# Depthwise conv taps on 32x32 tiles of TensorE, and 64-row score products in column halves

## The chip, the cores and the metric
One core of a Trainium2 chip runs the whole program. The metric is the device time of one execution in microseconds (us). Engines: TensorE (PE in the profile, its weight loads PEld), VectorE (DVE), ScalarE (ACT), GpSimd (POOL), and SyncE (SP), which issues the weight DMAs.

## What is computed
Two transformer blocks on a sequence of 512 tokens, width 1024, all in float32. The first has a hybrid mixer (differential attention with 4 heads of 2 x 64, and "fox" attention with 8 heads of 64 and a forget gate), cross attention to 256 memory tokens, and a squared-ReLU MLP. The second begins with the mixer that the change is about, then cross attention, a gated MLP with a three-tap conv, latent attention, cross attention again and a second gated MLP. The two parts that matter:

```python
def pool_conv_mixer(h, w_in, pool_w, pool_scale, dw_w, dw_b, ln_g, ln_b, w_out):
    z = h @ w_in
    u, glu_a, glu_b = jnp.split(z, [POOL_W, POOL_W + CONV_W], axis=-1)      # 512 each
    ...                                                                     # window means of u, @ pool_w -> ya
    gl = glu_a * jax.nn.sigmoid(glu_b)
    cv = causal_dwconv(gl, dw_w) + dw_b                                     # 31 taps, one channel each
    yb = jax.nn.silu(layernorm(cv, ln_g, ln_b))
    return jnp.concatenate([ya, yb], axis=-1) @ w_out
```

```python
s1 = jnp.einsum('bhqd,bhkd->bhqk', sl(qa1), ka1).astype(jnp.float32) * scale + rel    # d = 64, causal
s2 = jnp.einsum('bhqd,bhkd->bhqk', sl(qa2), ka2).astype(jnp.float32) * scale + rel
sb = jnp.einsum('bhqd,bhkd->bhqk', sl(qb), kb).astype(jnp.float32) * scale + ...      # fox, d = 64
```

## The kernel before
Everything lies feature-major: 128 features on the partitions, 512 tokens along the free axis. A dense product is split in three (mm3, L964): hi times hi, hi times lo, lo times hi of the operands, each a fast fp32r matmul of 512 columns. ScalarE writes the hi part of each 1 MB weight block (`hi`, L1628), GpSimd the lo part in four pieces (`low_part`, L810), SP loads the raw block two ahead. Other matmuls (scores, attention values, sums over features by a matrix of ones, conv taps) are plain f32.

Results go to PSUM through two rings of four banks each, L for dense products and S for the rest. `make_plan` writes down, in the order of the program, which engine frees each bank: "v" VectorE, "a" ScalarE. TensorE claims a bank (`claim`) when the group four places before has been read. There is no scheduler: each engine runs its instructions in the order in which its function writes them, and semaphores hold it where it must wait.

**The pool and conv mixer** is the stretch from about 950 to 1110 us. Its 512 conv channels are four chunks of 128 (`gl[:, q]`). A tap is a shift of the tokens times one weight per channel. TensorE does a tap of a whole chunk as a 128x128 diagonal matrix times the shifted chunk, summed in PSUM (L1470, L1485). VectorE does one as a fused multiply-add in SBUF (`taps`, L2783).
- Chunks 0 and 1: all 31 taps on VectorE. Chunk 2 (`SHARED_Q`): taps 0 to 14 on VectorE, 15 to 30 on TensorE ("conv2"). Chunk 3 (`PE_Q`): all on TensorE ("conv3"). So 77 taps on VectorE, 47 on TensorE. `tap_order` mixes VectorE's chunks, so that two taps of one chunk rarely follow one another.
- ScalarE makes the 47 diagonals (`diags` L2067, `shared_diags` L2074).
- TensorE's order: glu (8 groups of 128 features), pool_u (4 groups, two blocks), xk1+ (keys of the next cross attention, 256 columns), conv3, pool_w (4 products), conv2, first half of pc_out_a, ln_mean, second half, ln_var, memory values, pc_out_b. ln_mean (L1495) waits for all taps.
- VectorE's order: the glu scaling (`glu_in`, L2314), gates (`glu`, L2756), the normalised residual (L2763), scaled pool_u (L2314), the four window sums (L2803), means (L2808) and subtraction (L2811, which counts `pool_r` for pool_w), the lows of pool_w's results (L2818, for which pc_out_a waits), the closing adds of conv3 and conv2 (L2824, L2829). Taps stand between them.

The rows of the later sections also show L2884 (the three-tap conv of the gated MLP, whose taps wait each for the one before), L1601 (values of the latent attention: for each key tile k, two heads e, each a 128x64 product into its own half of a bank's partitions), L2157 (ScalarE's copy of 64 partitions out of PSUM) and L1309 (the causal mask, bf16, added by a matmul).

**The score products.** `diff_score` (L1263) and `masked_scores` (L1307) make two products at a time: head part 0 from partitions 0 to 63, part 1 from 64 to 127, each 64 rows x 128 columns of weights, moving 128 to 512 columns, into two banks. Each of the two attention stages has 16 such pairs, with dense products between them.

```python
            for j in range(CONV_K):
                pe.wait_ge(diag_r, j + 1)
                ins = pe.matmul(bank(S, g)[:, :], diag(j), gl[:, PE_Q, j:j + T], start=j == 0, stop=j == CONV_K - 1)
```

## Time and profile before

| | |
|---|---|
| median of 3 runs | 2385.51 us (2381.87 to 2385.61) |
| the profiled execution: its time, its span | 2383.48 us, 2381.6 us |
| granted TensorE clock, mean | 0.997 |
| PE busy | 2348.1 us (99%), 10762 matmul records |
| DVE, ACT, POOL busy | 1218.8, 939.8, 997.2 us |

The profile is one execution. A row of a timeline gives the start, the length up to the end of the last instruction of the group, engine, line, operation, output and inputs, shape and count. "128*128 128x512" is 128 rows by 128 columns of weights, and a moving operand of 128 partitions x 512 elements. Records of PE are pipelined: a matmul's record is longer than the step to the next one. A row of a list of groups ends with busy us and mean ns, then the engine's idle time before the group and what ended it.

### The profile page before, as it was taken

Reading aid. Unit: us, or ns where it says so; the run is one execution under the profiler, and the core shown is the slowest. Engines: PE = TensorE matmul, PEld = TensorE weight load, DVE = VectorE, ACT = ScalarE, POOL = GpSimd, SP = SyncE. Lnnn points to the kernel's source line nnn. Section 1 sums busy time; section 2 is a strip of 40 time slices with the busy share of each in tenths; the row PEclk is TensorE's granted clock in tenths of the full one; section 3 lists DMA queues with packets and bytes.
Section 4 is the critical chain, followed back from the end, with each engine's and each line's share of the span. In section 5 each row is a group of like instructions: output and inputs, shape, how many; then the busy total and the mean of one; then the engine's idle time right before and its main releaser. Section 6 shows DMA issues by size and latency. Waiting matters only on the chain.

```text
span 2381.6 us, 29066 instructions
## 1 busy us (share of the span) xinstructions
PE 2348.1 (99%) x10762; PEld 1864.9 (78%) x10762; DVE 1218.8 (51%) x2026; ACT 939.8 (39%) x1418; POOL 997.2 (42%) x744
## 2 busy tenths in 40 slices
PE   8999999999999999999999999999999999999999
PEld 6777778878888888757878888887667877888887
DVE  4454545244433346794457555556774243655544
ACT  3355444334222227424444222225875443322222
POOL 4323335223544545635525545444113233545443
PEclk9999999999999999999999999999999999999999
DMA  5212322422323223223213232222013521332231
...
DMA packets 170087, 218.69 MB, mean 92 GB/s; under 512 B 6585, under 2 KB 144107, under 8 KB 169975
## 3 DMA queue, kind: packets, MB, share of 16 engines
...
## 4 chain that ended last, share of the span: by engine, by line
PE 89%; DVE 4%; ACT 3%; issue 1%; POOL 1%; DMA 1%; SPq 0%; DVEq 0%; ACTq 0%
PE ps_l L964 79%; PE ps_l L1383 2%; PE ps_l L1113 1%; PE ps_s L1366 1%; ACT w_hi L1628 1%; POOL w_lo L810 1%; PE ps_s L1470 1%; DVE small L3025 1%; DVE arena L3017 1%; PE ps_s L1485 1%; PE ps_s L1263 1%; PE ps_s L1307 0%; PE ps_s L964 0%; DVE small L3027 0%; PE ps_l L1248 0%
## 5 line engine op out<-in xcount | busy, mean ns | idle before, releaser
L810 POOL TENSOR_TENSOR w_lo<-w_raw,w_hi 128x512 fp32r<-128x512 f32 (+1 forms) x740 | 997.0, 1378 | 1363.2 <-ACT w_hi L1628 1340.5
L964 PE MATMUL ps_l<-a_hi,w_hi 128*128 128x512 f32 x1936 | 762.9, 394 | 3.9 <-POOL w_lo L810 2.9
L964 PE MATMUL ps_l<-a_lo,w_hi 128*128 128x512 f32 x1952 | 758.4, 389 | 0.0
L964 PE MATMUL ps_l<-a_hi,w_lo 128*128 128x512 f32 x1936 | 754.0, 389 | 0.0
L1628 ACT ACTIVATE w_hi<-w_raw 128x2048 fp32r<-128x2048 f32 (+2 forms) x196 | 370.6, 1891 | 598.5 <-PE ps_l L964 575.7
L964 PEld LDWEIGHTS ps_l<-a_hi,w_hi 128*128 128x128 f32 x1936 | 362.7, 187 | 89.9 <-issue 10.9
L964 PEld LDWEIGHTS ps_l<-a_lo,w_hi 128*128 128x128 f32 x1952 | 365.9, 187 | 78.4 <-issue 3.1
L964 PEld LDWEIGHTS ps_l<-a_hi,w_lo 128*128 128x128 f32 x1936 | 362.7, 187 | 76.9
L964 PE MATMUL ps_l<-b_hi,w_hi 128*128 128x512 f32 (+1 forms) x892 | 330.3, 370 | 6.7 <-issue 2.3
L964 PE MATMUL ps_l<-b_lo,w_hi 128*128 128x512 f32 (+1 forms) x892 | 327.3, 367 | 0.0
L964 PE MATMUL ps_l<-b_hi,w_lo 128*128 128x512 f32 (+1 forms) x892 | 327.2, 367 | 0.0
L964 PEld LDWEIGHTS ps_l<-b_hi,w_hi 128*128 128x128 f32 x892 | 168.5, 189 | 38.0 <-issue 3.1
L964 PEld LDWEIGHTS ps_l<-b_hi,w_lo 128*128 128x128 f32 x892 | 168.6, 189 | 27.6
L964 PEld LDWEIGHTS ps_l<-b_lo,w_hi 128*128 128x128 f32 x892 | 168.6, 189 | 27.4 <-issue 0.2
L2910 DVE TENSOR_TENSOR x_T<-ps_l,x_T 128x512 f32<-128x512 f32 x160 | 109.3, 689 | 44.6 <-PE ps_l L964 42.6
L2314 DVE TENSOR_TENSOR arena<-ps_l,rst 128x512 f32<-128x512 f32 x56 | 38.2, 689 | 171.6 <-PE ps_l L964 114.9
L2715 DVE TENSOR_TENSOR x_T<-ps_l,x_T 128x512 f32<-128x512 f32 x120 | 82.9, 691 | 59.0 <-PE ps_l L964 58.0
L2627 DVE TENSOR_TENSOR x_T<-ps_l,x_T 128x512 f32<-128x512 f32 x64 | 43.5, 688 | 118.8 <-PE ps_l L964 118.5
L1660 ACT ACTIVATE a_hi<-x_T,cols 128x512 fp32r<-128x512 f32 x64 | 46.2, 723 | 141.4 <-DVE x_T L2627 141.4
L2875 DVE TENSOR_TENSOR arena<-ps_l,rst 128x512 f32<-128x512 f32 x44 | 30.4, 692 | 134.3 <-PE ps_l L964 121.2
L2691 DVE SCALAR_TENSOR_TENSOR arena<-ps_l,rst 128x512 f32<-128x512 f32 x32 | 22.0, 691 | 146.6 <-PE ps_l L964 137.3
L2884 DVE SCALAR_TENSOR_TENSOR arena<-arena,cols 128x512 f32<-128x512 f32 x88 | 91.3, 1038 | 8.4 <-DVE arena L2880 0.3
...
## 6 DMA issues: line engine op xcount, KB each, us to landing
...
```

Of the source, the lines that this page charges most:

```text
L810: e.tensor_tensor(w_lo[:, b % 2, o], w_raw[:, b % 2, o], w_hi[:, b % 2, o].bitcast(F32), ALU.subtract).then_inc(w_lo_made[by], 1)
L964: ins = pe.matmul(o, *((v, w) if swap else (w, v)), start=first and n == 0, stop=last and n == 2)
L1113: return pe.transpose(o, v, ident)
L1383: ins = pe.matmul(bank(L, g)[:, :], vM[:, m, h * 256 + d * P:h * 256 + (d + 1) * P], ptx(h)[:, m, :], start=m == 0, stop=m == MT - 1)
L1628: act.activation(w_hi[:, b % 2, 0:size], w_raw[:, b % 2, 0:size], ACT.Copy).then_inc(w_hi_made, 1)
L1660: act.activation(z_of(k)[0][:, n, :], x[:, n, :], ACT.Copy, scale=gain(k, n)).then_inc(n_hi, 1)
L2314: dve.tensor_tensor(dst(j), bank(L, g + j)[:, :], rst if r is None else r, ALU.mult)\
L2627: dve.tensor_tensor(x[:, n, :], bank(L, g)[:, :], x[:, n, :], ALU.add).then_inc(l_free["v"], 1)
L2715: dve.tensor_tensor(x[:, n, :], bank(L, g + n)[:, :], x[:, n, :], ALU.add)\
L2875: dve.tensor_tensor(gp[:, c, 2:T + 2], bank(L, g + c)[:, :], rst, ALU.mult)\
L2884: dve.scalar_tensor_tensor(out=cv[:, c, :], in0=gp[:, c, j:T + j], scalar=wcol(cw + 22 * j, k, i), in1=cv[:, c, :], op0=ALU.mult, op1=ALU. ...
L2910: dve.tensor_tensor(x[:, n, :], bank(L, g + n)[:, :], x[:, n, :], ALU.add)\
```

## The change
The conv: `tap_order` goes. VectorE keeps chunk 0 alone (31 taps in a row); TensorE takes chunks 1, 3 and 2, in this order, one before each pool_u block and one after them. A tap of a chunk is four f32 matmuls of 32 rows x 32 columns of weights, one for each 32 channels, whose diagonal blocks (`diag(n)`) VectorE builds for all 31 taps of a chunk in one instruction out of a 128x32 stack of small identities. Tap j sends channels 32r.. to bank s = (j+1) mod 4 and, in it, to the partitions of quarter (r + s) mod 4. So 16 matmuls in a row use 16 different tiles of the array, each with its own bank and quarter. The sum over the four banks and the way back to the right quarter is then made by ScalarE (12 copies of 32 partitions, banks 1 to 3, `conv_out`) and VectorE (`conv_add`, three adds). A chunk takes all four S banks; its adds come ahead of a given point of VectorE's order, and the copies for a chunk wait for the adds of the one before. ScalarE makes no diagonals any more.

The scores: both banks of a pair are claimed first; each 64x128 product becomes two of 64x64, for query columns 0 to 63 and 64 to 127.

```diff
--- before.py
+++ after.py
@@ -368,8 +368,8 @@
     feat("xk1+", "xa_wkv_2:0", "a", [768])
     L.add("pool_w", "vvvv")
     feat("pc_out_a", "pc_w_out_2", "v", [0, 512], nk=4, width=512)
-    S.add("conv3", "v")
-    S.add("conv2", "v")
+    for q in PE_CHUNKS:
+        S.add(f"conv{q}", "vaaa")
     S.add("ln_mean", "v")
     S.add("ln_var", "a")
...
@@ -424,27 +424,8 @@
...
-PE_Q = 3
-SHARED_Q, SHARED_TAPS = 2, 15
...
+DVE_CHUNK = 0
+PE_CHUNKS = (1, 3, 2)
...
@@ -677,10 +659,13 @@
         pool_wt = ar(12800, 4, P)
         ly = ar(R0, 4, T)
 
-        def diag(j):
-
-            o = P * j if j < 24 else R0 + 2168 + P * (j - 24)
-            return arena[:, o:o + P]
+        def diag(n):
+
+            return arena[:, 32 * CONV_K * n:32 * CONV_K * (n + 1)].rearrange("p (j c) -> p j c", c=32)
+
+        def conv_part(s):
+
+            return ar(10752 + T * (s - 1), T)
 
         qh, vh, kh = ar(R0, 8, T), ar(10752, 4, T), ar(HALF, 8, T)
         cosT, sinT = ar(12800, T), ar(13312, T)
@@ -1259,9 +1245,12 @@
                 n = P * (i + 1)
                 for s in (0, 1):
                     claim(pe, S, g + s)
+                for s in (0, 1):
                     r = slice(64 * s, 64 * s + 64)
-                    pe.matmul(bank(S, g + s)[:, 0:n], qa[r, h, i * P:(i + 1) * P], ka[r, h, 0:n],
-                              start=True, stop=True).then_inc(s_full, 1)
+                    for o in (0, 64):
+                        ins = pe.matmul(bank(S, g + s)[o:o + 64, 0:n], qa[r, h, i * P + o:i * P + o + 64], ka[r, h, 0:n],
+                                        start=True, stop=True)
+                    ins.then_inc(s_full, 1)
 
             def diff_subln(g, h):
                 claim(pe, S, g)
@@ -1302,9 +1291,11 @@
             def masked_scores(g, i, both):
 
                 n = P * (i + 1)
+                for e in (0, 1):
+                    claim(pe, S, g + e)
                 for e, (q, k) in enumerate(both):
-                    claim(pe, S, g + e)
-                    pe.matmul(bank(S, g + e)[:, 0:n], q, k[:, 0:n] if n < T else k, start=True, stop=False)
+                    for o in (0, 64):
+                        pe.matmul(bank(S, g + e)[o:o + 64, 0:n], q[:, o:o + 64], k[:, 0:n], start=True, stop=False)
                 for e in (0, 1):
                     pe.matmul(bank(S, g + e)[:, i * P:n], ident_bf[:, :], mask_bf[:, :], start=False, stop=True)\
                         .then_inc(s_full, 1)
@@ -1460,17 +1451,30 @@
...
             stage("glu", xa, ready=h_ready(4), behind={0: both_sums})
-            stage("pool_u", xa, nb=2)
+            def conv_taps(n):
+
+                q = PE_CHUNKS[n]
+                g = S.base[f"conv{q}"]
+                pe.wait_ge(glu_r, q + 1)
+                pe.wait_ge(diag_r, n + 1)
+                for s in range(4):
+                    claim(pe, S, g + s)
+                for j in range(CONV_K):
+                    s = (j + 1) % 4
+                    for r in range(4):
+                        rows, out = slice(32 * r, 32 * r + 32), 32 * ((r + s) % 4)
+                        ins = pe.matmul(bank(S, g + s)[out:out + 32, :], diag(n)[rows, j, :], gl[rows, q, j:j + T],
+                                        start=j < 4, stop=j >= CONV_K - 4)
+                    if j >= CONV_K - 4:
+                        ins.then_inc(s_full, 1)
+
+            b, g = plan.block_base["pool_u"], L.base["pool_u"]
+            conv_taps(0)
+            feat(b, g, 8, 256, xa)
+            conv_taps(1)
+            feat(b + 1, g + 2, 8, 256, xa)
+            conv_taps(2)
             stage("xk1+", xm, nb=1, n=MEM)
-            g = S.base["conv3"]
-            claim(pe, S, g)
-            pe.wait_ge(glu_r, 4)
-            for j in range(CONV_K):
-                pe.wait_ge(diag_r, j + 1)
...
@@ -1478,19 +1482,12 @@
...
-            g = S.base["conv2"]
-            claim(pe, S, g)
-            for j in range(SHARED_TAPS, CONV_K):
...
             feat(b, g, 4, 512, lambda k: xa(4 + k), lambda k: wait_read(pe, L, L.base["pool_w"] + k))
             g = S.base["ln_mean"]
             claim(pe, S, g)
-            pe.wait_ge(tap, TAPS)
-            wait_read(pe, S, S.base["conv2"])
+            pe.wait_ge(tap, CONV_K)
+            pe.wait_ge(conv_sum, len(PE_CHUNKS))
...
@@ -2059,20 +2056,20 @@
...
-            def diags():
-                for j in range(CONV_K):
...
+            def conv_out(n):
+
+                if n:
+                    act.wait_ge(conv_sum, n)
+                for s in (1, 2, 3):
+                    g = S.base[f"conv{PE_CHUNKS[n]}"] + s
+                    wait_group(act, S, g)
+                    for r in range(4):
+                        c = (r + s) % 4
+                        ins = act.activation(conv_part(s)[32 * r:32 * r + 32, :], bank(S, g)[32 * c:32 * c + 32, :], ACT.Copy)
+                    ins.then_inc(s_free["a"], 1)
+
+            for r in range(0, P, 32):
+                act.activation(part_id[r:r + 32, :], ident[r:r + 32, r:r + 32], ACT.Copy).then_inc(part_id_r, 1)
...
@@ -2081,10 +2078,13 @@
                     wait_read(act, L, g + 4 * pair + 2 + c)
                     act.activation(sgb[:, c, :], sgb[:, c, :], ACT.Sigmoid).then_inc(sg_r, 1)
                 hi(b + 2 * pair + 3)
-            diags()
-            just_hi("pool_u", 2)
+            b = plan.block_base["pool_u"]
+            conv_out(0)
+            hi(b + 2)
+            conv_out(1)
+            hi(b + 3)
+            conv_out(2)
             block_copies("xk1+", 1, 2, lambda j: kT[:, 6 + j, :], cols=MEM)
-            shared_diags()
             for q in range(4):
                 wait_group(act, L, L.base["pool_w"] + q)
                 act.activation(A_hi[:, 4 + q, :], bank(L, L.base["pool_w"] + q)[:, :], ACT.Copy,
@@ -2769,39 +2769,61 @@
...
             glu_in(1, 0)
+            dve.wait_ge(part_id_r, 4)
+            for n, q in enumerate(PE_CHUNKS):
+                w = COL["conv_dw_w_2"] + q
+                dve.tensor_tensor(diag(n), part_id.unsqueeze(1).broadcast_to((P, CONV_K, 32)),
+                                  cols[:, w:w + 4 * CONV_K - 3:4].unsqueeze(2).broadcast_to((P, CONV_K, 32)), ALU.mult)\
+                    .then_inc(diag_r, 1)
 
...
             def taps(upto):
-                for n in range(tap_n[0], min(upto, TAPS)):
-                    j, q, before = TAP_ORDER[n]
+                q = DVE_CHUNK
+                for j in range(tap_n[0], upto):
                     w = col("conv_dw_w_2", 4 * j + q)
                     if j == 0:
                         ins = dve.tensor_scalar(cvt[:, q, :], gl[:, q, 0:T], w, col("conv_dw_b_2", q), ALU.mult, ALU.add)
                     else:
-                        dve.wait_ge(tap, before + 1)
+                        dve.wait_ge(tap, j)
                         ins = dve.scalar_tensor_tensor(out=cvt[:, q, :], in0=gl[:, q, j:j + T], scalar=w,
                                                        in1=cvt[:, q, :], op0=ALU.mult, op1=ALU.add)
                     ins.then_inc(tap, 1)
-                tap_n[0] = max(tap_n[0], min(upto, TAPS))
+                tap_n[0] = upto
+
+            def conv_add(n):
+
+                q = PE_CHUNKS[n]
+                g = S.base[f"conv{q}"]
+                wait_group(dve, S, g)
+                wait_read(dve, S, g + 1)
+                dve.scalar_tensor_tensor(out=cvt[:, q, :], in0=bank(S, g)[:, :], scalar=col("conv_dw_b_2", q),
+                                         in1=conv_part(1), op0=ALU.add, op1=ALU.add).then_inc(s_free["v"], 1)
+                wait_read(dve, S, g)
+                wait_read(dve, S, g + 2)
+                dve.tensor_tensor(cvt[:, q, :], cvt[:, q, :], conv_part(2), ALU.add).then_inc(conv_acc, 1)
+                dve.wait_ge(conv_acc, n + 1)
+                wait_read(dve, S, g + 3)
+                dve.tensor_tensor(cvt[:, q, :], cvt[:, q, :], conv_part(3), ALU.add).then_inc(conv_sum, 1)
 
             glu(0)
-            taps(8)
             glu_in(1, 1)
-            taps(18)
+            taps(1)
             glu(1)
             normed_x(range(4, KD))
+            taps(4)
+            conv_add(0)
             scaled(L.base["pool_u"], 2, lambda j: up_[:, j, 16:UW], r34)
-            taps(26)
+            taps(12)
+            conv_add(1)
             scaled(L.base["pool_u"] + 2, 2, lambda j: up_[:, 2 + j, 16:UW], r34)
...
                 step(dve.tensor_tensor(dst[:, 0:m, st:UW], src[:, 0:m, st:UW], src[:, 0:m, st - d:UW - d], ALU.add))
-                taps(28 + 4 * (n + 1))
+                taps(12 + n + 1)
                 sync()
...
@@ -2810,7 +2832,8 @@
...
-            taps(60)
+            taps(20)
+            conv_add(2)
...
@@ -2818,17 +2841,7 @@
...
-            taps(TAPS)
-            g = S.base["conv3"]
...
+            taps(CONV_K)
             def pool_out(ns):
...
```

## Rows read from the trace of the kernel before

**Rows 1.** the page: span, busy time of the engines
```profile
span 2381.6 us, 29066 instructions
...
PE 2348.1 (99%) x10762; PEld 1864.9 (78%) x10762; DVE 1218.8 (51%) x2026; ACT 939.8 (39%) x1418; POOL 997.2 (42%) x744
```

**Rows 2.** busy time by stretches, pool projection to mean (columns: first line)
```profile
core 0: us, PE busy (x) PEld busy (x) DVE busy (x) ACT busy (x) POOL busy (x), PEclk, DMA share, GB/s
995.40:1023.60 28.20, 28.09 (x146) 23.40 (x145) 28.16 (x32) 16.23 (x37) 21.15 (x11) 1.00 0.31 105
...
1067.00:1078.30 11.30, 11.30 (x51) 9.18 (x50) 10.19 (x16) 0.00 (x0) 0.00 (x0) 1.00 0.00 0
sum 82.90, PE 82.79 PEld 51.73 DVE 81.72 ACT 27.25 POOL 32.45; mean PE 16.56 PEld 10.35 DVE 16.34 ACT 5.45 POOL 6.49
```

**Rows 3.** the list of waits, PE, 950 to 1130 us: total us, times, longest
```profile
PE ps_l L964 <- POOL w_lo L810: 0.8, 3, 0.3
```

**Rows 4.** timeline of PE: start us, us, line, op, tiles, count
```profile
1023.57 26.78 PE L1470 MATMUL ps_s<-arena 128*128 128x512 f32 x62
...
1053.62 13.90 PE L1485 MATMUL ps_s<-arena 128*128 128x512 f32 x32
1066.96 0.79 PE L964 MATMUL ps_l<-a_hi,w_hi 128*128 128x512 f32 x1
...
1078.25 3.17 PE L1495 MATMUL ps_s<-arena,ones 128*128 128x512 f32 x7
```

**Rows 5.** busy time of line L1601 alone, 1699.19 to 1701.50 us
```profile
1699.19:1701.50 2.31, 2.30 (x16) 1.06 (x16) 1.00 0.00 0
```

**Rows 6.** line L1601 at 1699.2 and to 1699.7: ns min/median/max, starts
```profile
L1601 PE MATMUL ps_l<-arena x2: 643/643/643, 1699.2 to 1699.2; 128*64 128x512 f32 x2
...
L1601 PE MATMUL ps_l<-arena x4: 592/618/643, 1699.2 to 1699.7; 128*64 128x512 f32 x4
```

**Rows 7.** line L1263, 95.13 to 95.2 and 95 to 95.5 us
```profile
L1263 PE MATMUL ps_s<-arena x2: 373/373/373, 95.1 to 95.1; 64*128 64x128 f32 x2
...
L1263 PE MATMUL ps_s<-arena x4: 272/322/373, 95.1 to 95.4; 64*128 64x128 f32 x4
```

**Rows 8.** timeline of PE around a score pair, 301 to 303.5 us
```profile
302.41 0.92 PE L1307 MATMUL ps_s<-arena 64*128 64x384 f32 x4
303.26 0.28 PE L1309 MATMUL ps_s<-mask_bf,ident_bf 128*128 128x128 bf16 x2
```

**Rows 9.** timeline of DVE, 979 to 1060 us
```profile
979.12 0.69 DVE L2314 TENSOR_TENSOR arena<-ps_l,arena 128x512 f32<-128x512 f32 x1 [1.52 <-PE ps_l L964]
984.56 0.69 DVE L2314 TENSOR_TENSOR arena<-ps_l,arena 128x512 f32<-128x512 f32 x1 [4.75 <-PE ps_l L964]
...
988.38 7.16 DVE L2783 SCALAR_TENSOR_TENSOR arena<-arena,cols 128x512 f32<-128x512 f32 x6
...
1049.52 10.68 DVE L2783 SCALAR_TENSOR_TENSOR arena<-arena,cols 128x512 f32<-128x512 f32 x16
```

**Rows 10.** groups by line and shape, DVE, 980 to 1080 us
```profile
L2811 DVE SCALAR_TENSOR_TENSOR arena<-arena 128x512 f32<-128x512 f32 x4 | 2.5, 687 | 0.0
...
L2803 DVE TENSOR_TENSOR arena<-arena 128x1042 f32<-128x1042 f32 x1 | 1.2, 1230 | 0.0
```

**Rows 11.** timeline of DVE in the gated MLP's three-tap conv
```profile
1390.21 1.65 DVE L2884 SCALAR_TENSOR_TENSOR arena<-arena,cols 128x512 f32<-128x512 f32 x2
```

**Rows 12.** busy time of line L2803, the window sums, 1025 to 1046 us
```profile
1025.00:1046.00 21.00, 7.11 (x4) 1.00 0.31 101
```

**Rows 13.** groups by line, ACT, 990 to 1095 us
```profile
L1628 ACT ACTIVATE w_hi<-w_raw 128x2048 fp32r<-128x2048 f32 x6 | 11.4, 1908 | 36.6 <-PE ps_l L964 36.6
L2067 ACT ACTIVATE arena<-keep,cols 128x128 f32<-128x128 f32 x31 | 9.2, 391 | 0.0
```

**Rows 14.** groups by line and shape, ACT, whole span
```profile
L2157 ACT ACTIVATE arena<-ps_l 64x512 f32<-64x512 f32 x16 | 9.5, 593 | 6.7 <-PE ps_l L964 6.6
```

**Rows 15.** the list of waits, PE, 60 to 330 us
```profile
PE ps_s L1263 <- ACT arena L1736: 0.4, 1, 0.4
```

44 lines of the change are left out of this document (3 added, 41 removed).

## Prediction

> **What bounds the kernel now.** The first part of the page shows TensorE (PE) busy 99% of a 2381.6 us span, the next engine 51% [rows 1]. So the kernel is TensorE's own stream of work, and an edit counts by what it takes out of that stream, as long as nothing else then holds it up. Next I read the busy time by stretches from the pool projection to the layer norm's mean [rows 2]. PE is busy in 82.8 of 82.9 us, at granted clock 1.00 (the 2.4 GHz level). What the page's averages hide is the DVE column: 81.7 of 82.9 us. In this stage two engines are full, and VectorE is the one that a faster PE would meet. The list of waits confirms that PE now waits for nothing there: 0.8 us in 180 us [rows 3]. The PE timeline gives the pieces: conv3 from 1023.57, conv2 from 1053.62, the first half of pc_out_a from 1066.96, ln_mean at 1078.25 [rows 4].
>
> **The convolution on PE.** 31 tap matmuls leave 62 records [rows 4]: an f32 matmul is two passes, each its own weight load and multiply. They run 26.78 us, of which the last lies 0.59 in its own, so the start-to-start of a 512-column pass is 26.2/61 = 0.43 us and a tap 0.86. Removed: conv3 62 x 0.43 = 26.6 and conv2 1053.62 to about 1067.1 = 13.5, together 40.1 us for 47 taps.
> Added: 93 taps in four 32x32 matmuls each, 372 matmuls, 744 passes and as many weight loads. Sixteen successive matmuls (four taps) lie on sixteen different tiles, so with all of them at work at once four taps cost 2 passes = 0.86 us. A chunk is 8 rounds: 6.9 us. Nothing in this trace uses 32x32 tiles; the nearest rows use two tiles. For the 128x64 products of the latent attention, 16 passes of 4 x (512+384+256+128) columns would take 4.3 us in a row at 0.43 per 512 and took 2.31, and the first two records, 512 columns each, start in the same 0.1 us [rows 5, 6]. They belong to two different matmuls, for a second pass of the first could not start before 0.43. Two 64-row tiles start together likewise [rows 7]. So both ways to split the array run side by side, at full rate, and a later matmul passes the second pass of an earlier one. I take that to hold for sixteen, with 0.5 us a chunk for emptying and filling at the change of tile shape (a 384-column score pair holds PE 0.85 us up to the mask, 2 x 0.32 of it streaming [rows 8]: 0.2 more, once on the way in and once out). Three chunks: 3 x 7.4 = 22.2 us. Off PE: 17.9 us. Lower bound of the cost: 20.6 (no overhead). Upper bound: only four row tiles side by side and the column quarters in turn, 93 x 0.86 = 80 us.
> The Trainium skill ("TensorE: Matmul & The Clock Gate", Part 3) reports 10.6 times one tile's rate for sixteen 32x32 tiles with 512 columns. The same section says that matmuls start and end in strict program order. By that rule the second pass of each matmul would hold back the next one, and the conv would cost 372 x 0.43 = 160 us; [rows 6] speak against it.
>
> **Where it runs into VectorE.** New order on PE: conv of chunk 1, pool_u block, chunk 3, pool_u block, chunk 2, xk1+, pool_w, pc_out_a. pool_u starts at 995.4 now (the glu group that VectorE takes at 984.56, plus two more of 5.44 us each [rows 9]). The stretch to conv3 is 28.2 us, so xk1+ would end at 995.4 + 28.2 + 22.2 = 1045.8 and pool_w (3.4, between conv3 and conv2) at 1049.2, whose first product needs the window sums.
> VectorE loses 46 of 77 taps. It gains three diagonal builds (992 elements each, priced by the 1042-element sum at 1.2 us [rows 10]; built at 985 to 990, five us ahead of PE), nine adds of 0.7, and loses two closing ops. But its 31 remaining taps all belong to one chunk, so each waits for the one before: chained taps of another stage run at 0.90 us (two in 1.65 with one of 0.75 [rows 11]) against 0.67 unchained (16 in 10.68 [rows 9]). While POOL works, tap times reach 1.2 (6 in 7.16 [rows 9]).
> DVE's course: all up to the first three taps is covered by waits for PE. It takes the last pool_u group when PE has it, 995.4 + 2 x 7.4 + 21.8 = 1032, done 1032.9. Then the four window sums, 7.1 [rows 12], four taps between them 3.6, subtraction 2.5 [rows 10] and about 0.3 for the means of a few columns: pool_r complete at 1046.4, about when PE comes to it. Then, ahead of the four pool lows, four taps (3.6) and conv_add(2) (3 chained ops, 2.7): 1052.7, and the first low at 1053.5. PE, free at 1049.2, waits for it: 4.3 us. pc_out_a's first half takes 11.3 [rows 2]: 1064.8. DVE: three more lows 2.1, eleven taps 9.9: 1065.5, with POOL working beside it for about 6 us (w_lo for pc_out_a's second block) 0.5 to 1.5 more. So ln_mean starts at about 1066.2 instead of 1078.25: **12 us** are kept and 6 of the 18 given back, to taps in a row. DVE's neighbours are covered from there on: the rest of the stage is unchanged in order.
>
> **ScalarE.** It loses 47 diagonals (31 of them took 9.2 us [rows 13]) and copies 3 x 12 pieces of 32x512 out of PSUM; the nearest row is a 64x512 copy from PSUM, 0.59 [rows 14], since the time goes by the 512 elements of a partition (128x512 ones of other lines are hardly longer): 12 are 7.1, with the first one's latency 7.3 us a chunk. Ends far apart are unlikely: half of it at a quarter of the partitions, or 0.7 each, 8.4. For chunk 1, PE ends it at 1002.8 and claims the banks again after 10.9 us of pool_u, at 1013.7; the copies are done at 1010.1. Chunk 3 ends at 1021.1, copied 1028.4, claimed 1032. Priced at nothing, cover 3.6 us each; without it PE would wait the difference. After chunk 2 (1039.4) they end at 1046.7, ahead of conv_add(2) at 1050. The w_hi splits queued behind them (1.9 us [rows 13]) fall after the blocks they wait for anyway. SP's and POOL's orders do not change. The four small copies for part_id come in ScalarE's idle time before the gates.
>
> **The score products.** 32 pairs of 64-row f32 products become four 64x64 tiles each. Same columns, same passes; if all four run together the streaming is equal and only the exposed first weight load shrinks: in the records the first pass with 128 columns of weights runs 373 ns against 272 for the next [rows 7], and with 64 columns 643 against 592 [rows 6], so 50 ns less. 32 x 0.05 = **1.6 us**, on PE's path since PE is full there. Bounds: a gain of 3.2 (the load gone), a loss of one more pass pair of mean 320 columns, 0.53 x 32 = 17 us, if only two run together. Claiming both banks ahead of the first product: PE's wait at these lines was 0.4 us in both attention stages [rows 15]; VectorE frees the pair's banks one right behind the other. Nothing.
>
> **Sum.** 12.0 + 1.6 = 13.6 us off the profiled execution's 2383.48, i.e. 2369.9. The median of the runs is 2385.51, 2.0 above it: **2371.9**. 0.2% (4.8 us) is about what a measurement of this kernel can tell from no change.
>
> **Rivals.**
> A, the forecast, 0.62. Own range 2367 to 2377: DVE giving back 2 more to all but 9 us, scores 0 to 3.
> B, sixteen tiles overlap only in part, for instance eight at a time because the pass pairs fill what PE can look ahead to: conv 3 x (13.7+0.5) = 42.6, +2.5 on PE; DVE, with 20 us more time, no longer makes PE wait. With eight 2386, with twelve about 2377. For it: no row shows more than two tiles. 0.13, half of it at either end.
> C, the instruction stream. 744 load-multiply pairs must be issued, and if a pair costs over 40.1/744 = 54 ns the conv is a loss whatever the array could do. The shortest pitch in the trace is two bf16 masks of 128 columns, 0.28 for both with 0.22 for one: 60 ns [rows 8]. At that rate 44.6 us: 2385.5 + 4.5 - 1.6 = 2388.4. Against it: the pitch of these is also their 128 columns (0.053), so it need not be an issue rate, and the two tiles of [rows 6] start within one tick. 0.10, half of it at 65 ns and more, which is measurably slower (48 us, 2392).
> The skill's same page ("Wait — 56ns, not 53.3ns?") gives about 62 ns per matmul where the sequencer decodes in software, 46 us here, and about 25 ns otherwise; no run here tells which.
> D, **slower**: row tiles overlap, but the four column quarters of one row tile take turns, since all four read the same 32 partitions, each at its own shift, where the rows show two readers at most. Then the conv is 93 x 0.86 = 80 us, VectorE is far ahead, and the time 2385.5 + 40 - 1.6 = 2424. It decides from the third reader on: with two at a time it is case B at eight. Against it: two readers cost nothing [rows 5, 6]. 0.09.
> E, strict order of passes: a pass 2 holds back the next matmul, one matmul per 0.43 us, 160 us, 2504. Against it: [rows 6]. 0.02. This is the page's rule above.
> F, the score quarters run two at a time: 17 us lost, 2390. 0.04.
>
> **How the numbers follow.** Faster: A and the better half of B, 0.69, say 0.70. Same: the worse half of B and the milder of C, 0.11, say 0.10. Slower: half of C, D, E, F, 0.20. The range takes A, B and the milder half of C, 0.80: from 2366 (a point below A's range) to 2389. The forecast is A's.
>
> **What would show it.** Right: 744 conv records at 32*32 whose three stretches last about 7.4 us each; sixteen starts within a fraction of one pass; PE waiting 3 to 6 us ahead of pc_out_a for a DVE low and up to 2 at ln_mean for the last tap; taps at 0.9 us pitch; ln_mean 12 us earlier after the start of pool_u; score stretches 50 ns shorter. Wrong: conv stretches of 13 us or more (B, C: the gap between starts tells them apart, even at 55 to 60 ns for C), 27 us (D), 53 us (E); a wait of PE for ScalarE's copies at a conv's start; a granted clock below 1.00 in a conv stretch.

## The result, and the profile after

| | before | after |
|---|---|---|
| median | 2383.69 us of 4 runs (2380.47 to 2385.61) | 2396.24 us of 4 runs (2395.3 to 2397.69) |
| profiled execution: span | 2381.6 us [rows 1] | 2394.0 us |

The ratio is 1.0056, with a 95% interval from 1.0044 to 1.0069. The change makes the kernel slower by 12.6 us; the forecast was 13.6 faster. The first part of the page of the changed kernel:

```profile
span 2394.0 us, 30628 instructions
PE 2353.1 (98%) x11540; PEld 1858.7 (78%) x11540; DVE 1196.7 (50%) x1990; ACT 946.0 (40%) x1411; POOL 994.1 (42%) x744
```

Lines of the changed kernel: L950 is the dense product (L964 before), L1466 the conv taps on PE, L1483 pool_w, L1492 ln_mean, L2789 VectorE's taps, L2825 the window sums, L2841 the pool lows, L2068 ScalarE's copies, L796 GpSimd's low parts.

PE is still the bound, and its busy time has risen from 2348.1 us [rows 1] to 2353.1, although some 14 us of conv work are gone. So I cut both traces at the same points of the program (the first record on PE of the sum or transposition that opens each stage) and compared the lengths:

| stretch of the program | before, us | after, us | difference |
|---|---|---|---|
| start to mlp, with both score stages | 586.0 | 586.1 | +0.1 |
| mlp | 327.3 | 332.2 | **+4.9** |
| memory keys, glu projection | 45.8 | 45.8 | 0.0 |
| pool and conv mixer, to the next norm | 193.1 | 187.7 | **-5.5** |
| cross attention 1 | 120.6 | 121.6 | +1.1 |
| ffn0 | 365.7 | 372.4 | **+6.6** |
| latent attention | 264.1 | 261.6 | -2.5 |
| cross attention 2 | 120.6 | 121.6 | +1.1 |
| ffn1, to the end | 358.4 | 365.0 | **+6.6** |

The differences add up to the 12.4 us between the spans. The changed part is faster, if by less than forecast. What makes the kernel slower is five stretches of which the diff touches no instruction: +20.3 us in them. In the first row a gain by the scores is cancelled likewise: the stages behind the score stages start 0.94 us sooner (384.09 before, 383.15 after), and the first cross attention, between 465 and 586 us, then loses 1.1.

**What is slow in the untouched loops.** The timeline of PE, one whole turn between two kinds of products in the mlp loop. Columns: start us, length us, engine, line, operation, tiles, count. First the kernel before:

```profile
630.41 0.39 PE L964 MATMUL ps_l<-a_hi,w_hi 128*128 128x512 f32 x1
...
641.29 0.39 PE L964 MATMUL ps_l<-b_hi,w_hi 128*128 128x512 f32 x1
```

and the kernel after:

```profile
620.24 0.39 PE L950 MATMUL ps_l<-b_hi,w_hi 128*128 128x512 f32 x1
...
631.14 0.40 PE L950 MATMUL ps_l<-a_hi,w_hi 128*128 128x512 f32 x1
...
642.33 0.39 PE L950 MATMUL ps_l<-b_hi,w_hi 128*128 128x512 f32 x1
```

Between a first a_hi and the next b_hi lie 48 passes of the "up" products, between a first b_hi and the next a_hi 48 of the "down" products. Up: 10.88 us before, 11.19 after, a pitch (start to start) of 226.7 and 233.1 ns. Down: 10.90 us after, 227.1 ns a pass. PE waits for nothing in either; the same instruction with the same shape takes 3% longer if its operand is the a of this loop. That a is not the a_hi/a_lo of the attention stages but the second pair, a2_hi/a2_lo (the profile leaves the 2 out of its name). Over the whole trace, the mean pitch of a-products is 227.0 ns before and 230.8 after; times 5824 passes that is 22 us. Cross attention's query products use a2 too.

**What moved.** The change has one more tensor in SBUF, `part_id` (128 partitions x 128 bytes), allocated ahead of the arena and a2. So a2_hi, which lay 95232 = 372 x 256 bytes behind w_hi, lies 95360 behind it. This is the one thing that differs for these products.

**The stage that was meant.** The timeline of PE in the pool stage after, which answers to [rows 4]:

```profile
1000.30 8.63 PE L1466 MATMUL ps_s<-arena 32*32 32x512 f32 x248
1019.96 8.63 PE L1466 MATMUL ps_s<-arena 32*32 32x512 f32 x248
1039.63 8.62 PE L1466 MATMUL ps_s<-arena 32*32 32x512 f32 x248
1054.23 3.67 PE L1483 MATMUL ps_l<-arena 128*128 128x512 f32 x8
...
1064.84 0.77 PE L950 MATMUL ps_l<-a_hi,w_hi 128*128 128x512 f32 x1 [6.94 <-DVE a_lo L2841]
...
1077.49 1.88 PE L1492 MATMUL ps_s<-arena,ones 128*128 128x512 f32 x4
```

```profile
L1466 PE MATMUL ps_s<-arena x16: 612/612/613, 1000.3 to 1000.4; 32*32 32x512 f32 x16
```

This row is from the list of line L1466 (ns min/median/max, first and last start): sixteen passes start within 0.10 us, and the next sixteen 0.45 us after them. So sixteen tiles do work side by side. A chunk takes 8.6 us instead of the forecast 7.4. The starts of the second chunk tell where the excess lies: a round of sixteen matmuls (32 passes) begins every 1.07 us (7.52 us for seven rounds), where two passes of 0.43 make 0.86. The 0.21 us in between come with every round, not once a chunk. PE then waits 6.94 us for VectorE's first pool low (forecast 4.3). The windows (columns as in [rows 2]) show what follows that wait:

```profile
1055.00:1062.00 7.00, 2.90 (x7) 0.95 (x5) 6.86 (x8) 4.48 (x7) 4.75 (x4) 0.97 0.00 0
1062.00:1068.00 6.00, 3.16 (x8) 2.52 (x9) 5.93 (x8) 0.00 (x0) 1.52 (x1) 0.50 0.53 173
1068.00:1078.00 10.00, 10.00 (x44) 8.09 (x43) 9.21 (x14) 0.25 (x1) 0.00 (x0) 0.98 0.01 3
```

Granted clock 0.50, the 1.2 GHz level, from 1061.6 to 1068.4: it falls while PE waits (1057.9 to 1064.8) and comes back 3.6 us after the work does. So the first passes of pc_out_a run at 430 ns a pitch instead of 227, about 1.8 us lost. ln_mean starts 77.2 us after the stage's start (1000.30), where it was 82.9 [rows 2].

VectorE's timeline shows why the low is late, and GpSimd's what ran beside it:

```profile
1039.73 0.69 DVE L2314 TENSOR_TENSOR arena<-ps_l,arena 128x512 f32<-128x512 f32 x1 [3.32 <-PE ps_l L950]
1040.46 2.35 DVE L2825 TENSOR_TENSOR arena<-arena 128x2108 f32<-128x2108 f32 x1
1042.73 1.77 DVE L2789 SCALAR_TENSOR_TENSOR arena<-arena,cols 128x512 f32<-128x512 f32 x1
1044.43 2.87 DVE L2825 TENSOR_TENSOR arena<-arena 128x1575 f32<-128x1575 f32 x1
...
1055.81 4.93 DVE L2789 SCALAR_TENSOR_TENSOR arena<-arena,cols 128x512 f32<-128x512 f32 x4
...
1064.00 2.71 DVE L2841 SCALAR_TENSOR_TENSOR a_lo<-ps_l,cols,a_hi 128x512 fp32r<-128x512 f32 x4
1066.63 8.61 DVE L2789 SCALAR_TENSOR_TENSOR arena<-arena,cols 128x512 f32<-128x512 f32 x11
```

```profile
1041.78 8.34 POOL L796 TENSOR_TENSOR w_lo<-w_raw,w_hi 128x512 fp32r<-128x512 f32 x4 [13.35 <-ACT w_hi L1625]
1057.25 6.28 POOL L796 TENSOR_TENSOR w_lo<-w_raw,w_hi 128x512 fp32r<-128x512 f32 x4 [7.12 <-ACT w_hi L1625]
```

From the end of VectorE's last pool_u group to the end of its first low 24.3 us pass (1040.42 to 1064.73); the forecast had 20.6. The four taps of this stretch that lie beside GpSimd's weight splitting take 1.64 to 1.77 us each (the group of four in 4.93 holds two of them and two of 0.75); with GpSimd idle, eleven chained taps take 8.61, 0.78 each. The kernel before has the same meeting the other way round:

```profile
999.29 6.43 POOL L810 TENSOR_TENSOR w_lo<-w_raw,w_hi 128x512 fp32r<-128x512 f32 x1 [6.29 <-ACT w_hi L1628]
```

This one piece takes 6.43 us, where most of this stage take 1.3 to 1.9, while six taps and two gate products of VectorE pass at 0.69 to 0.75 each. So where the two meet, one of them is held up; no run took either away, so this is read from the traces alone. ScalarE's copies are as forecast, and hidden:

```profile
1008.50 7.24 ACT L2068 ACTIVATE arena<-ps_s 32x512 f32<-32x512 f32 x12 [4.94 <-PE ps_s L1466]
```

### The profile page after: what moved, and what is told of

The parts are those of the page before. It is cut to its first block, busy times and chain, and to the rows that moved or that the text cites. A ratio compares the mean times of both kernels' runs of the same rounds, so it can differ in the third digit from the quotient of the medians.

```text
span 2394.0 us, 30628 instructions
## 1 busy us (share of the span) xinstructions
PE 2353.1 (98%) x11540; PEld 1858.7 (78%) x11540; DVE 1196.7 (50%) x1990; ACT 946.0 (40%) x1411; POOL 994.1 (42%) x744
## 4 chain that ended last, share of the span: by engine, by line
PE 90%; DVE 5%; ACT 3%; issue 1%; DMA 1%; POOL 1%; SPq 0%; DVEq 0%; ACTq 0%
PE ps_l L950 80%; PE ps_l L1374 2%; PE ps_l L1099 1%; PE ps_s L1357 1%; ACT w_hi L1625 1%; DVE small L3038 1%; POOL w_lo L796 1%; DVE arena L3030 1%; PE ps_s L1466 1%; PE ps_s L1251 0%; PE ps_s L1298 0%; PE ps_s L950 0%; DVE small L3040 0%; PE ps_l L1598 0%; PE ps_l L1234 0%
## 5 line engine op out<-in xcount | busy, mean ns | idle before, releaser
L796 POOL TENSOR_TENSOR w_lo<-w_raw,w_hi 128x512 fp32r<-128x512 f32 (+1 forms) x740 | 993.9, 1375 | 1378.7 <-ACT w_hi L1625 1360.5
L950 PE MATMUL ps_l<-a_hi,w_hi 128*128 128x512 f32 x1936 | 769.9, 398 | 10.8 <-DVE a_lo L2841 6.9
L950 PE MATMUL ps_l<-a_lo,w_hi 128*128 128x512 f32 x1952 | 765.7, 393 | 0.0
L950 PE MATMUL ps_l<-a_hi,w_lo 128*128 128x512 f32 x1936 | 761.1, 393 | 0.0
L950 PEld LDWEIGHTS ps_l<-a_hi,w_hi 128*128 128x128 f32 x1936 | 363.4, 188 | 104.9 <-issue 11.0
L950 PEld LDWEIGHTS ps_l<-a_lo,w_hi 128*128 128x128 f32 x1952 | 366.6, 188 | 85.6 <-issue 2.9
L950 PEld LDWEIGHTS ps_l<-a_hi,w_lo 128*128 128x128 f32 x1936 | 363.3, 188 | 84.1
L950 PE MATMUL ps_l<-b_hi,w_hi 128*128 128x512 f32 (+1 forms) x892 | 329.8, 370 | 6.3 <-issue 2.3
L950 PE MATMUL ps_l<-b_hi,w_lo 128*128 128x512 f32 (+1 forms) x892 | 326.9, 366 | 0.0
L950 PE MATMUL ps_l<-b_lo,w_hi 128*128 128x512 f32 (+1 forms) x892 | 326.9, 366 | 0.0
L950 PEld LDWEIGHTS ps_l<-b_hi,w_hi 128*128 128x128 f32 x892 | 168.1, 188 | 38.7 <-issue 4.4
L950 PEld LDWEIGHTS ps_l<-b_lo,w_hi 128*128 128x128 f32 x892 | 168.2, 189 | 27.6 <-issue 0.2
L950 PEld LDWEIGHTS ps_l<-b_hi,w_lo 128*128 128x128 f32 x892 | 168.1, 189 | 27.6
L2314 DVE TENSOR_TENSOR arena<-ps_l,rst 128x512 f32<-128x512 f32 x56 | 38.2, 689 | 174.6 <-PE ps_l L950 117.0
L2888 DVE TENSOR_TENSOR arena<-ps_l,rst 128x512 f32<-128x512 f32 x44 | 30.4, 691 | 143.2 <-PE ps_l L950 129.6
L2906 DVE TENSOR_TENSOR arena<-ps_l,rst 128x512 f32<-128x512 f32 x44 | 30.3, 691 | 132.3 <-PE ps_l L950 132.3
```

Source lines behind the costliest of these rows:

```text
L796: e.tensor_tensor(w_lo[:, b % 2, o], w_raw[:, b % 2, o], w_hi[:, b % 2, o].bitcast(F32), ALU.subtract).then_inc(w_lo_made[by], 1)
L950: ins = pe.matmul(o, *((v, w) if swap else (w, v)), start=first and n == 0, stop=last and n == 2)
L2314: dve.tensor_tensor(dst(j), bank(L, g + j)[:, :], rst if r is None else r, ALU.mult)\
L2888: dve.tensor_tensor(gp[:, c, 2:T + 2], bank(L, g + c)[:, :], rst, ALU.mult)\
L2906: dve.tensor_tensor(f32[:, c, :], bank(L, g + 2 + c)[:, :], rst, ALU.mult)\
```

## The experiments

The first four ask whether the address is the cause. Each "pad" is a tensor that nothing reads or writes.

**e1_pad_before**, the kernel before and one line behind the allocation of `ck8`:
```diff
+        sb("pad", [P, 32])
```


> The kernel before, with one unused tensor of 128 bytes a partition where the changed kernel has its identity tiles; not one instruction is added. Theory (address): the change is slow because a2_hi and a2_lo lie 128 bytes further on, so that each dense product that reads them takes 0.233 us instead of 0.2266; 3456 of them give +22 us, so 2404 to 2407 us, with the same longer pitch in the mlp and ffn loops and in the cross queries. Rival (the conv change itself, its longer PE instruction stream or its pattern of tiles slows the later loops): no tile and no instruction changes here, so 2384 us, the same. Second rival (the window of operands of ScalarE or VectorE beside PE): also the same.

Measured: 2405.18 us, ratio 1.0091 [1.0075, 1.0107], 21.8 us slower by a line that adds no instruction. The mlp loop, one turn of 48 down and 48 up passes:

```profile
623.54 0.39 PE L965 MATMUL ps_l<-b_hi,w_hi 128*128 128x512 f32 x1
...
634.44 0.40 PE L965 MATMUL ps_l<-a_hi,w_hi 128*128 128x512 f32 x1
...
645.63 0.39 PE L965 MATMUL ps_l<-b_hi,w_hi 128*128 128x512 f32 x1
```

10.90 and 11.19 us, as in the changed kernel. The theory holds; the conv is not needed for the loss.

**e3_part_last**, the changed kernel with `part_id` allocated last:
```diff
         ck8 = sb("ck8", [P, TT * 8])[:, :]
-        part_id = sb("part_id", [P, 32])[:, :]
...
         bf_col = sb("forget_bias", [8, 1])[:, :]
+        part_id = sb("part_id", [P, 32])[:, :]
```


> The changed kernel with its 128-byte identity tensor put behind all others, so that every other tensor lies where it lies in the kernel before; all instructions stay. Theory (address): pitch of the products on a2 back to 0.2266 us, time 2396.2 less 22 = 2374 us, some 9.5 us under the kernel before (5.6 by the pool stage, 1.9 by the scores, the rest in the latent attention). Rival (the conv change's own instructions do it): 2396, slower than before by 12.

Measured: 2375.82 us, ratio 0.9969 [0.9959, 0.9979]. Same instructions as the changed kernel and 20.4 us faster; mlp, ffn0, ffn1 and both cross attentions are back to the lengths of before within 0.1 us. (Its profiled execution, 2376.1 us long, lies only 5.5 under that of before: the start-up, up to the first sum over features, is 1.8 us longer in it; it differs by 2 us between v2 and v4 below, which share all of its code and all addresses.) The wait in the pool stage stays:

```profile
PE ps_l L950 <- DVE a_lo L2841: 6.9, 1, 6.9
```

So what the change's instructions do by themselves is worth 7.5 us of gain.

**e4_scores_only**, the kernel before with the diff's two score hunks alone.


> The kernel before with the score products split into column halves alone; no tensor moves. The forecast gave this part 1.6 us; the changed kernel's trace shows the stages behind the two score stages starting 0.94 and 1.0 us sooner. So 1 to 2 us under the kernel before, 2382. Rival (the split is what slowed the later loops): 2404, with the a2 pitch at 0.233.

Measured: 2380.87 us, ratio 0.9994 [0.9984, 1.0003]. The rival falls; the gain can't be told from no change by the times. In its trace 287.96 us lie between the first score pair and the stage behind both score stages, in the changed kernel's 287.99, in that of before 288.95. The two figures that I had added up in the expectation, 0.94 and 1.0, are one gain seen at two later points. So 1.0 us of the 1.6 forecast, 31 ns a pair and not 50.

**p64_pad256**, as e1 with `[P, 64]`.


> The kernel before with an unused tensor of 256 bytes a partition at the same place; a2_hi then lies at 128 modulo 256 as before, but at 384 modulo 512 instead of 128. If what counts is the address modulo 256: 2384, the same. If it is the address modulo 512, or the distance to tensors that lie ahead of the pad (the weights): some of the 22 us, 2390 to 2407.

Measured: 2383.25 us, ratio 1.0 [0.9991, 1.001]. Twice the pad costs nothing. So it is no matter of how far the tensors move, but of a residue, modulo 256 and not 512.

The next runs ask which distance counts, and how.

**pf_pad_front**, the kernel before with the pad of 128 bytes ahead of all tensors:
```diff
+        sb("pad", [P, 32])
         x = sb("x_T", [P, KD, T])
```


> The kernel before with an unused tensor of 128 bytes a partition ahead of all others, so that x, a_hi/lo, b_hi/lo, the weights and a2_hi/lo all lie 128 bytes further on (0 modulo 256 instead of 128). Theory 1 (the moving operand's own address counts: 0 modulo 256 is the slower one): all dense products, on a, b and a2, go at 0.233 instead of 0.2266; with about 8600 of them some 57 us more, 2440. Theory 2 (the distance of the moving operand to the weights or to another tensor that lies ahead of the pad): all distances but those to PSUM are as before, 2384, the same. In between: only the products on a2 slow, 2405 (then something about that end of the memory counts).

Measured: 2383.99 us, ratio 0.9999 [0.9989, 1.0008]. a2 lies at the very address at which it was slow in e1, and is fast; nor are a and b slower. An address by itself is not it: theory 2.

**pw_pad_weights**, the pad between `b_lo` and `w_raw`.


> The kernel before with the unused 128-byte tensor between b_lo and w_raw: a2 and the split weights are shifted together, a_hi/lo and b_hi/lo are not. With the pad ahead of everything, a2 lay at the very address that is slow elsewhere and was fast, so an address by itself is not it. Theory (what counts is the distance modulo 256 of the moving operand to the weights): products on a2 at 0.2266, those on a and b (about 4400) at 0.233: 2384 + 29 = 2410 to 2413. Rival 1 (distance of a2 to a, b or x, that is to what the other engines write meanwhile): a2 at 0.233, a and b at 0.2266, 2405. Rival 2 (something in the arena's distance): 2384.

Measured: 2405.57 us, ratio 1.0095 [1.0079, 1.011]. The mlp loop, which is now the other way round:

```profile
626.56 0.40 PE L965 MATMUL ps_l<-b_hi,w_hi 128*128 128x512 f32 x1
...
637.75 0.39 PE L965 MATMUL ps_l<-a_hi,w_hi 128*128 128x512 f32 x1
...
648.65 0.40 PE L965 MATMUL ps_l<-b_hi,w_hi 128*128 128x512 f32 x1
```

The 48 b-passes take 11.19 us and the 48 on a2 10.90. The slow products changed places when the weights moved: the distance between the moving operand and the weights is what counts. The time came out 4 to 7 us lower than my count of passes on a and b gave.

**pl_pad_wlo**, the pad between `w_hi` and `w_lo`.


> The kernel before with the unused 128-byte tensor between w_hi and w_lo: w_lo and a2 lie at 0 modulo 256, w_hi, a and b at 128. Each product is three passes: hi on w_hi, lo on w_hi, hi on w_lo, and while one pass streams, the weights of the next are loaded. If the distance to the weights being loaded counts: for a2 the pass before a load of w_hi is slow (2 of 3) and for a and b the one before a load of w_lo (1 of 3); about 3456 x 2/3 + 4400 x 1/3 = 3770 slow passes, +25 us, 2408. If it is the pass's own weights: a2 slow in 2 of 3, a and b in 1 of 3, the same sum but in the next pass of the row, which the pitches tell apart. Rival (no relation to the weights): 2405 with all three a2 passes alike and a, b untouched.

Measured: 2423.57 us, ratio 1.0166 [1.015, 1.0181]. More than either form of the theory gave. Passes on b in a row:

```profile
630.24 0.39 PE L966 MATMUL ps_l<-b_hi,w_hi 128*128 128x512 f32 x1
630.47 0.40 PE L966 MATMUL ps_l<-b_lo,w_hi 128*128 128x512 f32 x1
630.70 0.40 PE L966 MATMUL ps_l<-b_hi,w_lo 128*128 128x512 f32 x1
630.94 0.39 PE L966 MATMUL ps_l<-b_hi,w_hi 128*128 128x512 f32 x1
631.16 0.40 PE L966 MATMUL ps_l<-b_lo,w_hi 128*128 128x512 f32 x1
```

Means over the loop: 227.4 ns from the first pass to the second (both on w_hi), 232.2 to the third (w_lo is loaded meanwhile), 234.0 from it to the next first. For a2, whose residue is that of w_lo, all three are slow (232.7, 232.0, 234.5), although its pass on w_lo fits. So it is neither the pass's own weights alone nor those loaded meanwhile alone: a pitch was short only where the moving operand agreed with both.

**pm_pad_whi** tests that, with pads of 128 bytes ahead of `w_hi` and ahead of `w_lo`.


> The kernel before with unused tensors of 128 bytes ahead of w_hi and ahead of w_lo: only w_hi lies at 0 modulo 256, while w_lo, a, b and a2 lie at 128. With w_lo and a2 moved, the pitches had spared only the pair of passes in which both passes' operands and weights agreed. Theory (a pitch is short only if the operands and the weights of both neighbouring passes agree modulo 256): each of the three pitches of every dense product has w_hi on one side or the other, so all are slow, on a, b and a2 alike: 7850 x 6.5 ns = 51 us, less some that waits hide, 2425 to 2435. Rival 1 (only a pass's own operand and weights count): the pass on w_lo is spared, 2 of 3 slow, 34 us, 2416. Rival 2 (a shift of w_hi costs nothing, what counts is a2 and w_lo): 2384.

Measured: 2432.38 us, ratio 1.0206 [1.0189, 1.0223]. All pitches are slow, on a2 and b alike: 232.2, 232.8, 235.0 ns. The rule stood its test.

**p16_pad64** and **p48_pad192**, as e1 with `[P, 16]` and `[P, 48]`.


> The kernel before with an unused tensor of 64 bytes a partition at the place of the changed kernel's identity tensor: a2 shifted by 64 against the weights. If any distance that is no multiple of 128 or 256 is slow: 2405. If the slow case needs exactly 128: 2384. If the cost grows with the distance: about half, 2394.

> The kernel before with an unused tensor of 192 bytes at the place of the changed kernel's identity tensor. 64 bytes cost 9 us, 128 cost 22, 256 nothing. Theory (the cost repeats with 256 and is symmetric about 128): as at 64, 2390 to 2394. Rival (it depends on the distance in one direction only): as at 128, 2405, or nothing, 2384.

Measured: 2392.32 us, ratio 1.0041 [1.0025, 1.0056], and 2404.81, ratio 1.0087 [1.007, 1.0103]. At 64 bytes the three pitches on a2 are 231.6, 226.5 and 229.5, at 192 they are 233.6, 233.0 and 233.4. The cost comes back to nothing at 256, but is not symmetric about 128: my expectation for 192 was wrong, and its rival (as at 128, 2405) came out. All of them together (residues modulo 256; mean pitch in the mlp loop, ns, where two passes differ all three):

| kernel | w_hi, w_lo | a and b | a2 | pitch on b | pitch on a2 | against before |
|---|---|---|---|---|---|---|
| before | 128, 128 | 128 | 128 | 226.6 | 226.6 | |
| after; e1 | 128, 128 | 128 | 0 | 227.0 | 233.2 | +12.6; +21.8 |
| e3 | 128, 128 | 128 | 128 | 226.7 | 226.7 | -7.5 |
| p64 | 128, 128 | 128 | 128 | 226.6 | 226.6 | -0.1 |
| pf | 0, 0 | 0 | 0 | 226.7 | 226.7 | +1.5 |
| pw | 0, 0 | 128 | 0 | 233.2 | 227.0 | +22.3 |
| p16 | 128, 128 | 128 | 192 | 227.6 | 231.6, 226.5, 229.5 | +9.1 |
| p48 | 128, 128 | 128 | 64 | 227.1 | 233.4 | +21.2 |
| pl | 128, 0 | 128 | 0 | 227, 232, 234 | 233, 232, 235 | +40.3 |
| pm | 0, 128 | 128 | 128 | 232, 233, 235 | 232, 233, 235 | +48.7 |

The last column is between medians, in us, each against the runs of before on the same chip; of pf's 1.5 nothing can be told from no change.

The other runs are about the pool stage, all on top of e3.

**v2_lows_first**, on VectorE:
```diff
-            taps(20)
-            conv_add(2)
             for q in range(4):
                 g = L.base["pool_w"] + q
...
                     .then_inc(l_free["v"], 1)
+            taps(20)
+            conv_add(2)
             taps(CONV_K)
```


> The changed kernel with its identity tensor last, and on DVE the four low parts of the pool output ahead of four taps and the last sum of the conv parts. In the trace PE waits 6.9 us for the first of these lows and then runs 6.8 us at half its clock. Theory (that order is what gave back part of the 18 us): the 6.9 us wait falls below 1 us, the clock stays at 1.0, but ln_mean then waits 4 to 5 us for the last tap: net 2 to 4 us under the version without it, 2372 to 2374. Rival (DVE's sum of work sets ln_mean whatever its order): 2376, the same.

Measured: 2379.28 us, ratio 0.9986 [0.9976, 0.9995], some 3 us slower than e3 and above both expectations. PE's waits in the stage:

```profile
PE ps_s L1492 <- issue: 9.2, 1, 9.2
PE ps_l L950 <- POOL w_lo L796: 2.8, 5, 1.3
PE ps_l L950 <- DVE a_lo L2839: 0.8, 1, 0.8
```

The 6.9 us are gone as expected, but 9.2 appear at ln_mean (twice what I expected). The profile names no releaser ("issue"); VectorE's last tap ends at 1072.69 and ln_mean starts at 1072.79, so it is the taps that it waits for. The clock is at 0.50 for 10.2 us from within that wait on, and the stage is 3.6 us longer than in e3. The wait moved, and grew.

**v3_mean_later**, on top of v2: ln_mean behind two of the four products of pc_out_a's second half, and `pool_out((n,))` after each of `taps(24)`, `taps(26)`, `taps(28)`, `taps(31)`.


> The one before, and ln_mean behind two of the four products of pc_out_a's second half, with the sums into x one by one between the taps. PE then has 6.5 us more of its own work to do while DVE ends the taps, and 6.7 us behind ln_mean to cover the squares. Theory: both waits gone, 5 to 8 us under the changed kernel with its tensor last, 2368 to 2371, and about 14 us under the kernel before, near the 12 kept of 18 plus 1.6 that the forecast had counted. Rival: ln_var now waits for VectorE's subtraction and ScalarE's squares, 2374 to 2377.

Measured: 2375.91 us, ratio 0.9965 [0.9954, 0.9977]: e3's time, and the stage to within 0.1 us e3's length. The theory of 2368 to 2371 fails.

```profile
PE ps_s L1495 <- issue: 3.4, 1, 3.4
PE ps_l L950 <- POOL w_lo L796: 2.8, 5, 1.3
PE ps_l L950 <- DVE a_lo L2843: 0.8, 1, 0.8
PE ps_l L950 <- DVE x_T L2852: 0.7, 1, 0.7
```

The windows (columns as in [rows 2]) show a second cost behind the 3.4 us of waiting:

```profile
1075.00:1081.00 6.00, 6.00 (x7) 2.44 (x8) 0.47 (x1) 0.00 (x0) 0.00 (x0) 0.50 0.44 169
```

The clock is at 0.50 from 1074.2 to 1081.0, and 6.0 us of PE's work run at it, which costs some 3 us. So the new order brings nothing in sum: VectorE is busy without a gap from 1053 to 1075, PE still waits for its last tap, and then pays for the clock. What is left is the work that VectorE still has there.

**v4_taps_early**, on top of e3, moves that work ahead into VectorE's idle time:
```diff
             normed_x(range(4, KD))
-            taps(4)
+            taps(12)
             conv_add(0)
             scaled(L.base["pool_u"], 2, lambda j: up_[:, j, 16:UW], r34)
-            taps(12)
+            taps(25)
             conv_add(1)
+            taps(28)
...
-                taps(12 + n + 1)
+                taps(min(28 + n + 1, CONV_K))
...
-            taps(20)
             conv_add(2)
...
-            taps(CONV_K)
```


> The changed kernel with its identity tensor last, with PE's order as it was, and the DVE taps placed where its trace shows DVE idle: taps 5 to 12 ahead of the first sum of conv parts, 13 to 25 ahead of the second, 26 to 28 ahead of the second pool_u pair, the last three between the window sums, and the third sum of parts ahead of the pool lows. In the trace of the version without it DVE idles some 12 us between 1002 and 1036 for PE and ScalarE and has 15 taps (13.5 us) still to do when the window sums are over. Theory (the work left to DVE behind the window sums is what kept only 5.6 us of 18): PE's wait for the first low falls from 6.9 to about 1 us, its clock stays at 1.0, ln_mean comes 7 to 8 us sooner, 2366 to 2369 us. Rival (DVE's total or the ScalarE copies set the stage, as moving the lows alone and ln_mean alone brought nothing): 2374 to 2376.

Measured: 2368.06 us, ratio 0.9934 [0.9921, 0.9948]: within the 2366 to 2369 of the theory, 7.8 us under e3, 15.2 under the kernel before and 28.2 under the changed one (the medians of the kernel before lie within 1.2 us of each other in all comparisons). VectorE's timeline and PE's waits:

```profile
1002.87 10.55 DVE L2789 SCALAR_TENSOR_TENSOR arena<-arena,cols 128x512 f32<-128x512 f32 x11
1013.34 0.75 DVE L2800 SCALAR_TENSOR_TENSOR arena<-ps_s,cols,arena 128x512 f32<-128x512 f32 x1
...
1016.65 13.76 DVE L2789 SCALAR_TENSOR_TENSOR arena<-arena,cols 128x512 f32<-128x512 f32 x13
...
1053.39 2.73 DVE L2841 SCALAR_TENSOR_TENSOR a_lo<-ps_l,cols,a_hi 128x512 fp32r<-128x512 f32 x4 [0.37 <-ACT a_hi L2090]
1063.50 2.67 DVE L2848 TENSOR_TENSOR x_T<-ps_l,x_T 128x512 f32<-128x512 f32 x4 [7.38 <-PE ps_l L950]
```

```profile
PE ps_l L950 <- DVE a_lo L2841: 1.1, 1, 1.1
PE ps_l L950 <- POOL w_lo L796: 0.8, 3, 0.4
```

VectorE now waits for PE behind the lows (7.38 us) instead of PE for VectorE, the clock is 1.00 in the whole stage, and the stage is 7.6 us shorter than in e3, 13.4 than in the kernel before.

**e6_conv_halves** asks what makes a chunk 8.6 us instead of 7.4 (indentation shortened):
```diff
-                for j in range(CONV_K):
+                for c in (0, 256):
+                    for j in range(CONV_K):
...
-  ins = pe.matmul(bank(S, g + s)[out:out + 32, :], diag(n)[rows, j, :], gl[rows, q, j:j + T],
+  ins = pe.matmul(bank(S, g + s)[out:out + 32, c:c + 256], diag(n)[rows, j, :],
+                  gl[rows, q, j + c:j + c + 256],
```


> On top of the changed kernel with its identity tensor last: each chunk's 31 taps go over columns 0 to 255 first and over 256 to 511 then, so twice as many load-and-multiply pairs stream the same number of columns. A chunk took 8.6 us for 248 pairs, 34.8 ns a pair. If the column work of the sixteen tiles sets it (the forecast's 6.9 us and some overhead), a chunk stays at 8.6 to 9 us and the kernel at 2376. Rival (the forecast's third: the stream of pairs sets it, only at 35 ns a pair instead of the 54 to 60 feared): 496 pairs take 17.3 us a chunk, 26 us more on PE before the DVE chain, of which some 20 reach the end: 2396.

Measured, in a single execution: 2381.87 us beside a median of 2382.54 for the kernel before, too little to compare the times by. The stage is 8.7 us longer than in e3. The second chunk on PE's timeline:

```profile
1021.93 6.14 PE L1467 MATMUL ps_s<-arena 32*32 32x256 f32 x283
1029.02 2.75 PE L1467 MATMUL ps_s<-arena 32*32 32x256 f32 x128 [0.95 <-issue]
1032.75 2.03 PE L1467 MATMUL ps_s<-arena 32*32 32x256 f32 x85 [0.98 <-issue]
```

496 pairs take 12.9 us with 1.9 us of gaps in it, 22 ns a pair outside the gaps and 26 with them. Both theories fail: a pair can follow in 22 ns, so the 34.8 of the full-width chunk is not the limit of the instruction stream; but column work alone would not have gone from 8.6 to 12.9. The starts say more. Outside the gaps a round of sixteen half-width matmuls begins every 0.65 us; two passes of half the columns are 0.43 (an estimate, from 0.43 us for one of 512 columns). So a round costs 0.22 us above its column work here and 0.21 at full width, and 7.75 rounds make that 1.6 to 1.7 us a chunk, the excess over the forecast's 6.9. What PE does in these 0.2 us, and what the gaps are, stays open. The first chunk has 3.4 us at clock 0.50 in it, from 1001.7 on, behind a gap of 2.3 us; no other run has a clock below 1.00 in a conv stretch.

## Why the prediction was wrong

**The step that failed is a term that the sum left out, at nothing and without a reason.** The sum counted what the change's instructions cost and save, stage by stage, and left every other product at its time of before. The diff has a term that is no instruction: `part_id`, 128 bytes a partition, allocated ahead of a2. Its price was 20.4 us (e3 against the changed kernel), or 21.8 alone (e1), in stages that the prediction never looked at. None of the rivals is this one: B to F all lie in the changed instructions, and the slower one, D, has the column quarters take turns, which the timeline refutes (8.6 us a chunk, not 27). Without this term (e3) the change gains 7.5 us of the 13.6 forecast: 2375.8 against a kernel before at 2383.4, where the forecast went from 2385.5 to 2371.9. That e3 falls into the stated range does not make the rest of the sum right; the points below say what was mis-sized in it.

What the Trainium skill says would have led away from it. "TensorE: Matmul & The Clock Gate", Part 2, "Step-by-step: what each phase is for", holds that loading the next weights takes no SBUF bandwidth from the running matmul, since TensorE has two read ports. The rows here differ by 3% with the distance between the two operands, and pl_pad_wlo shows that the weights loaded meanwhile count (on b and w_hi, 227.4 ns ahead of a pass on w_hi, 232.2 ahead of one on w_lo). So the measurement decides: the two do disturb each other, at some distances. Why, no run here shows.

**Point by point.**
- *Sixteen tiles at work at once*: right. 744 records in three stretches of 8.6 us, sixteen starts within 0.10 us; rivals B (13.7), D (27) and E (53) are out. The size was off: 25.9 us for 22.2. The term for filling and emptying was put at 0.5 us once a chunk; it is 0.21 us with every round of sixteen, 1.7 a chunk. Rival C's 54 to 65 ns a pair is out too: 34.8 here and 22 in e6.
- *VectorE's first low is late, 4.3 us*: right in place, 6.9 in size. The course from the last pool_u group to the low was 24.3 us, not 20.6: 3.7 us more, while PE came 1.2 later (the longer chunk). GpSimd's weight splitting runs beside a good part of it, and the forecast had priced taps and sums there without it. Chained taps alone were cheaper than priced (0.78, not 0.90), so the forecast 1.4 us of waiting at ln_mean did not come.
- *A clock below 1.00 there*: not foreseen. 6.8 us at the 1.2 GHz level, of which 3.6 with work, cost some 1.8 us. This wait of 6.9 us cost more than itself.
- *12 us kept of 18*: 5.5 (changed kernel) and 5.8 (e3). 3.7 more for the conv, 2.6 more of waiting and 1.8 by the clock, less the 1.4, make 6.7; 6.2 to 6.5 are missing. "Six given back to taps in a row" was the right mechanism: v4 takes those taps out of the way, and the stage is then 13.4 us shorter than before.
- *Scores 1.6 us*: 1.0 in the traces, by itself not to be told from no change (e4). Rival F's loss of 17 us is out.
- *ScalarE's copies 7.3 us a chunk, hidden; no wait at a conv's start*: right, 7.24, and no such wait.
- The latent attention is 2.5 us shorter after. PE has 3.4 us at half clock there against 10.2 before; this varies between kernels that share all of that code (6.8 in v4, none in e6), so I lay it to no part of the change.
